# Two edits to a decoder-step kernel: query products of the even layer turned round, and expert panels parted by the contraction

## What is computed

```
q_in = qc * jnp.exp(b)
o_inter = jnp.einsum('bchk,bhkv->bchv', q_in, S)
att = jnp.einsum('bthk,bshk->bhts', q_in, k_in)
o_intra = jnp.einsum('bhts,bshv->bthv', att, vc)
return S_new, o_inter + o_intra
```

## Time and profile before

| | |
|---|---|
| median of 3 runs | 1671.39 us (1671.09 to 1671.58) |
| the profiled execution, own time | 1670.99 us |
| its span, first to last instruction | 1669.2 us |
| PE busy | 1587.6 us (95%) |
| DVE, ACT, POOL busy | 539.7, 341.4, 144.6 us |
| mean granted TensorE clock | 0.983 |
| mean DMA rate | 321 GB/s |

### The profile page before, as it was taken

The page is one execution under the profiler, slowest core; times in us unless marked ns, Lnnn a source line. Parts: engine busy times, 40 slices in busy tenths (PEclk is TensorE's granted clock), DMA queues, the critical chain, the costliest instruction groups (busy, mean ns, idle before and its releaser), DMA issues.

```text
span 1669.2 us, 21844 instructions
## 1 busy us (share of the span) xinstructions
PE 1587.6 (95%) x7954; PEld 799.2 (48%) x7954; DVE 539.7 (32%) x1322; ACT 341.4 (20%) x693; POOL 144.6 (9%) x221
## 2 busy tenths in 40 slices
PE   8999899999999999999999999989999999999998
PEld 5784544334344433446665755554443434443343
DVE  2145722222222222261434245372222222222225
ACT  2102122121122221231222222012212112221122
POOL 0330100000000000000011111010000000000000
PEclk9969999999999999999999999989999999999999
DMA  9623779999989999955385586577999998999970
GB/s 299 245 82 133 277 313 419 421 421 420 420 348 421 420 420 420 388 200 188 134 269 195 196 279 235 202 310 306 421 421 421 420 419 362 420 421 419 421 291 29
DMA packets 119271, 536.09 MB, mean 321 GB/s; under 512 B 17849, under 2 KB 29369, under 8 KB 69408
## 3 DMA queue, kind: packets, MB, share of 16 engines
q1 hardware_dynamic: 95975, 470.35, 70.5%
q0 software_dynamic: 21360, 61.64, 10.2%
q10 hardware_dynamic: 1872, 3.22, 0.6%
HBM read 526.15 MB, written 23.87 MB: 330 GB/s over the span
## 4 chain that ended last, share of the span: by engine, by line
PE 81%; DMA 11%; DVE 3%; issue 2%; ACT 1%; SPq 1%; POOL 0%; ACTq 0%; DVEq 0%
PE ps L1252 23%; PE ps L1116 12%; PE ps L1094 12%; DMA weights<-in_w_exp_up 11%; PE ps L1266 10%; PE ps L1228 5%; PE ps L1245 3%; PE ps L1224 2%; PE ps L1259 1%; PE ps L1010 1%; PE ps L1105 1%; PE ps L1286 1%; PE ps L988 1%; PE ps L901 1%; PE ps L1001 1%
## 5 line engine op out<-in xcount | busy, mean ns | idle before, releaser
L1252 PE MATMUL ps<-weights,x_feat 128*64 128x512 f32 x1984 | 437.8, 593 | 36.8 <-DMA weights<-in_w_exp_up 18.5
L1252 PEld LDWEIGHTS ps<-weights,x_feat 128*64 128x64 f32 x1984 | 147.1, 137 | 320.9 <-issue 318.2
L1266 PE MATMUL ps<-weights,arena 128*64 128x512 f32 x992 | 226.5, 598 | 0.9 <-ACT arena L1450 0.9
L1094 PE MATMUL ps<-x_feat,weights 128*128 128x288 f32 x832 | 210.2, 411 | 1.1 <-ACT x_feat L1450 1.1
L1094 PEld LDWEIGHTS ps<-x_feat,weights 128*128 128x128 f32 x832 | 159.9, 194 | 45.1 <-issue 3.8
L2104 DVE CAST split<-state 128x1024 fp32r<-128x1024 f32 (+1 forms) x66 | 44.7, 678 | 324.9 <-ACT state L1450 324.9
L2101 DVE SCALAR_TENSOR_TENSOR arena<-arena,ps 128x256 f32<-128x256 f32 x64 | 30.7, 480 | 365.3 <-ACT arena L1679 365.3
L2423 POOL DMA_INDIRECT arena<-x_rows,arena x64 | 63.6, 993 | 891.0 <-DVE arena L2094 845.9
L1450 ACT ACTIVATE state<-ps 128x512 f32<-128x512 f32 x132 | 78.8, 597 | 268.5 <-PE ps L1266 261.1
L1116 PE MATMUL ps<-weights,x_feat 128*128 128x512 f32 x288 | 126.7, 594 | 3.0 <-ACT x_feat L1476 3.0
L1266 PEld LDWEIGHTS ps<-weights,arena 128*64 128x64 f32 x992 | 65.7, 136 | 132.3 <-issue 130.9
(11 more groups left out here) (289 smaller groups left out, 1280.8 us busy)
## 6 DMA issues: line engine op xcount, KB each, us to landing
weights<-in_w_exp_gate SPq DMA_DIRECT2D x124, 1024.0 KB, 14.8
weights<-in_w_exp_up SPq DMA_DIRECT2D x124, 1024.0 KB, 18.8
weights<-in_w_exp_down SPq DMA_DIRECT2D x124, 1024.0 KB, 16.9
weights<-in_w_in_c SPq DMA_DIRECT2D x24, 1024.0 KB, 8.1
arena<-in_state_ret POOLq DMA_DIRECT2D x20, 512.0 KB, 5.5
out_ret_sample<-arena POOLq DMA_DIRECT2D x20, 512.0 KB, 6.5
weights<-in_w_in_a SPq DMA_DIRECT2D x8, 1024.0 KB, 10.9
weights<-in_w_ple_gate SPq DMA_DIRECT2D x8, 1024.0 KB, 17.8
```

The costliest lines, as they stand in the source:

```text
L1094: last = pe.matmul(ps[:, 0:T], lhs(c), XT[:, c, :], start=(c == 0), stop=(c == n - 1))
L1252: last = pe.matmul(ps[64 * s:64 * s + 64, :], XGT[u][:, c, 64 * s:64 * s + 64], rhs, start=(c == 0), stop=(c == KC - 1))
L1266: last = pe.matmul(ps[64 * s:64 * s + 64, :], HT[u][:, c, 64 * s:64 * s + 64], wd[s][:, c, 512 * n:512 * n + 512], start=(c == 0), stop=(c ...
```

## The change

Two parts.

**A, even layer.** The queries of a chunk become the stationary operand (QI is laid out chunk by chunk, so that the 32 columns lie together) and the state the moving one, 128 columns. Four chunks write four strips of 32 output partitions of one bank. There are 32 such products for the prompt (the first chunk's state is set to zero by a POOL memset and takes part) and 16 for the samples: groups ("qS", 0), ("qS", 1), ("qSs"). ACT copies each bank to SBUF (for the samples with a factor 0 or 1 for each row, from a new table column `own_strip`). The pooling products follow. Then ("oT", f) takes its four products of scores and values and four more of 128 x 128 by the identity, which turn the copied result and add it; ("oTs") takes its four and four more with a folding matrix.

**B, expert loop.** For the first and the last pair of each layer, panels 0 and 1 hold the first and the second half of the contraction of all four matrices, in runs of 4 KB where the other panels have 8 KB. `gate_up_halves` waits for one panel, does 8 products, waits for the next, does 8 more. At the first pair it signals after the first half, and SP refills that slot then. SP's first loop iteration is written out for this.

```diff
+            g.extend((("qS", 0), ("qS", 1), ("qSs",)))
+            g.extend(("pool", f) for f in range(4))
             g.extend((("oT", 0), ("oT", 1), ("oTs",)))
-            g.extend(("pool", f) for f in range(4))
...
+                def contraction_panel(num, e0, k):
+                    s = slot_full[num % SLOTS]
+                    dst = wp(num).rearrange("p (s m x) -> p s m x", s=2, m=2)
+                    for m, w in enumerate((A["w_exp_gate"], A["w_exp_up"])):
+                        src = w[l, e0:e0 + 2].rearrange("e (p c) n -> p e (c n)", c=KC)
+                        sp.dma_start(dst[:, :, m, :], src[:, :, 1024 * k:1024 * k + 1024]).then_inc(s, 16)
...
                             if k == 2:
                                 sp.wait_ge(bank_full[1], base[1] + 3 * (u - 1 + late) + 6 * it)
+                            elif isinstance(it, int) and it == 1 and u + k == 0:
+                                sp.wait_ge(sem("half_consumed"), l + 1)
                             else:
                                 sp.wait_ge(bank_full[0], base[0] + 2 * (u + late) - 3 + 4 * it)
-                            expert_panel(n0 + 3 * u + k, 4 * it + 2 * u, k)
+                            if isinstance(it, int) and it > 1 and k < 2:
+                                contraction_panel(n0 + 6 * it + k, 4 * it, k)
+                            else:
+                                expert_panel(n0 + 3 * u + k, 4 * it + 2 * u, k)
...
             for f in range(2):
-                for i in range(1, NCA):
-                    pe.matmul(out2[:, :, CA * i:CA * i + CA], SS[:, f, i, :], QI[:, f, :, CA * i:CA * i + CA],
-                              start=(i == 1), stop=False, skip_group_check=True)
+                ps = begin(("qS", f))
+                for i in range(NCA):
+                    q, g = i % 4, i // 4
+                    last = pe.matmul(ps[TS * q:TS * q + TS, P * g:P * g + P], QI[:, f, i].rearrange("p k c -> p (k c)"), SS[:, f, i, :],
+                                     start=(g == 0), stop=(g == 3), skip_group_check=True)
+                end(last, ("qS", f))
...
             for f in range(2):
+                out2 = begin(("oT", f)).rearrange("p (k t) -> p k t", k=2)
...
+                emptied(pe, ("qS", f))
+                for g in range(4):
+                    tokens_of = out2[:, :, 64 * g:64 * g + 64].rearrange("p k (i c) -> p i k c", c=CA)
+                    last = pe.matmul(tokens_of, QS[f][:, P * g:P * g + P], ident, start=False, stop=(g == 3),
+                                     skip_group_check=True)
                 end(last, ("oT", f))
...
+            emptied(pe, ("qSs",))
+            for f in range(2):
+                for g in range(2):
+                    last = pe.matmul(out4[:, 2 * f:2 * f + 2, CA * g:CA * g + CA], QSS[:, P * (2 * f + g):P * (2 * f + g) + P],
+                                     fold_all[:, 0:TS], start=False, stop=(f == 1 and g == 1), skip_group_check=True)
             end(last, ("oTs",))
...
+                def gate_up_halves(u, ring, it, ps):
+                    for k in range(2):
+                        n = ring + k
+                        pe.wait_ge(slot_full[n % SLOTS], 32 * (n // SLOTS + 1) + 32 * it)
+                        w = wp(n).rearrange("p (s m c n) -> p s m c n", s=2, m=2, c=4)
+                        for c in range(4):
+                            for s in range(2):
+                                last = pe.matmul(ps[64 * s:64 * s + 64, :], XGT[u][:, 4 * k + c, 64 * s:64 * s + 64],
+                                                 w[:, s, :, c, :], start=(k == 0 and c == 0), stop=(k == 1 and c == 3))
+                        if it == 0 and k == 0:
+                            last.then_inc(sem("half_consumed"), 1)
+                    return last
...
+                    for f in range(2):
+                        full(act, ("qS", f))
+                        st.free(copy(QS[f], bank(("qS", f))), ("qS", f))
+                    full(act, ("qSs",))
+                    st.free(copy(QSS, bank(("qSs",)), scale=own_strip), ("qSs",))
```

More of the change, by code:

```diff
@@ L430, in trunk @@
         AT = XTb[:, 4 * T:8 * T].rearrange("p (h t) -> p h t", h=4)
+        QS = [STATE[:, 512 * f:512 * f + 512] for f in range(2)]
+        QSS = keys[:, 0:512]
         a = Cut(AR[:, :], ASZ)
@@ L763, in _, with two_pairs @@
                         wait_slot(n0 + 3 * pr + k)
-                        expert_panel(n0 + 3 * pr + k, 2 * pr, k)
+                        if pr == 0 and k < 2:
+                            contraction_panel(k + n0, 0, k)
+                        else:
+                            expert_panel(n0 + 3 * pr + k, 2 * pr, k)
                 sp.wait_ge(sem("flag_ready"), l + 1)
                 go = sp.value_load(flagi[0:1, 0:1], min_val=0, max_val=1)
-                def two_pairs(it, late):
-                    for u in range(1 if isinstance(it, int) else 2):
+                def two_pairs(it, late, pairs=2):
+                    for u in range(pairs):
                         for k in range(3):
@@ L887, in even_pe @@
                 for j, (o, r) in enumerate(CH):
-                    last = pe.matmul(ps[0:r, o:o + r], KI[:, h // 2, o:o + r], QI[:, h // 2, h % 2, o:o + r],
-                                     start=True, stop=True)
+                    last = pe.matmul(ps[0:r, o:o + r], KI[:, h // 2, o:o + r],
+                                     QI[:, h // 2, o // CA:(o + r) // CA, h % 2, :], start=True, stop=True)
                 end(last, ("att", h))
@@ L1316, in two_pairs @@
                             pe.wait_ge(sem("home_in"), 96 * (l + 1))
-                        else:
+                        elif not (first or last):
                             for n in range(ring, ring + 2):
@@ L1320, in two_pairs @@
                         pe.wait_ge(bank_free[0], base[0] + uses(0, pr, 0))
-                        gate_up(u, HOME_UP if home else [wp(ring), wp(ring + 1)], PS[:, 0, :]).then_inc(bank_full[0], 1)
+                        if first or last:
+                            gate_up_halves(u, ring, it, PS[:, 0, :]).then_inc(bank_full[0], 1)
+                        else:
+                            gate_up(u, HOME_UP if home else [wp(ring), wp(ring + 1)], PS[:, 0, :]).then_inc(bank_full[0], 1)
                         pe.wait_ge(bank_free[1], base[1] + uses(1, pr, 0))
@@ L1792, in even_dve @@
                         dve.wait_ge(sem("queries_zeroed"), 1)
-                    st.run(STT(QI[0:64, f, 0, :], ps[0:64], DKA ** -0.5, EB[0:64, f, :], ALU.mult, ALU.mult))
-                    st.free(STT(QI[64:128, f, 1, :], ps[64:128], DKA ** -0.5, EB[64:128, f, :], ALU.mult, ALU.mult), ("qk", f))
+                    for k in range(2):
+                        rows = slice(64 * k, 64 * k + 64)
+                        ins = STT(QI[rows, f, :, k, :], ps[rows].rearrange("p (i c) -> p i c", c=CA), DKA ** -0.5,
+                                  EB[rows, f, :].rearrange("p (i c) -> p i c", c=CA), ALU.mult, ALU.mult)
+                        if k:
+                            st.free(ins, ("qk", f))
+                        else:
+                            st.run(ins)
                 else:
@@ L2328, in even_pool @@
             store(O["pool_sample"][0, :, 0:PBUF - DSEQ, :], A["state_pool"][0, :, DSEQ:PBUF, :], s)
+            st.run(pool.memset(SS[:, :, 0, :], 0.0))
+            st.after
             st.tell(pool.memset(QI, 0.0), sem("queries_zeroed"))
```

35 lines of the change are left out of this document (19 added, 16 removed).

## The result

The changed kernel takes 1656.95 us (median of 4 runs, 1655.94 to 1657.13), the kernel before 1671.24 beside it: a ratio of 0.991, interval 0.990 to 0.993. The forecast was 1649.0 with a range to 1655.5: the direction is right, but 8 us of the 22.4 are missing. The profiled execution took 1657.13 us, span 1655.2 (before 1669.2).

The account below looks back on a forecast made before the run. PE bounds nearly all; in the expert loop the weight stream's start does. 13.1 + 2 x 3.1 + 1.6 + 1.5 = 22.4 us off 1670.99 gives 1648.6, plus 0.4: 1649.0 us, range 1646.5 to 1655.5.

Parts of the forecast that it names:

- Part A: Even layer, query products to oTs: products turned round in strips, with pooling and folds, gain 13.1 us.
- Rival 2: Even layer: the clock returns early, around 107 us, 1.4 us better, 1647.6 us; chance 10%.
- The copies: Even layer: ACT's three copies of 0.60 us each, done at 110.3 before the first fold needs them, cost nothing.
- First pair: Expert loop's start: refill issued 3.5 us earlier, gain 3.1 us a layer, between 0 and 3.5.
- Rival 3: Expert loop: the stream runs dry at 230.7 us, losing the early refill's gain; 6.2 us worse, 1655.2 us; chance 13%.
- Last pair: Expert loop's end: gate_up starts without idle time before it, gain 1.6 us, and 1.5 in layer 1.
- the sum: Whole kernel: 13.1 + 2 x 3.1 + 1.6 + 1.5 = 22.4 us gained, all reaching the end.
- What was to show it wrong: Pooling starting after 112 us, clock 0.50 at the output projection, or home pair's gate_up less than 2 us earlier.
- rivals outside the range (4 and 5): Clock stays low after the even layer's products, 1687.7 us, 2%; strips don't overlap and extra folds cost, 1665 us, 5%.
- theory 1: Posed after the result: at layer 0's loop end PE waits for its own instructions at the overflow branch, about 7 us.
- theory 4: Posed after the result: three added groups shift later PSUM banks, costing time before layer 0's loop and at the odd layer.

Follow-up runs that it names:

- e11: Changed kernel with 48 instructions less in TensorE's never-entered overflow routine, so only the branch's target moves; 1650.50 us, ratio 0.988.
- e1: Changed kernel without TensorE's branch over the overflow routine and the routine's body; 1650.44 us, ratio 0.988 to the kernel before.
- e7: Kernel before with 56 instructions (112 waits on the second constant transfer) at the head of TensorE's program; 1696.31 us, ratio 1.016.
- e15: Changed kernel with PSUM banks turned back by five at layer 0's router and 32 instructions of waits in PE's idle time ahead of it; 1647.08 us, ratio 0.985.
- e8: Changed kernel with banks turned back at the output projection and 64 instructions (waits on the second constant transfer) at the program's head; 1667.22 us, ratio 0.998.
- e9: Changed kernel with banks turned back at layer 0's router and 64 instructions (waits on the identity's semaphore) at the program's head; 1651.90 us, ratio 0.989.
- e13: Changed kernel with PSUM banks turned back by five at layer 0's router, nothing else; 1653.63 us, ratio 0.989 to the kernel before.
- e5: Changed kernel with the PSUM bank rotation skipping five at the first group of the output projection; 1655.13 us, ratio 0.991 to the kernel before.
- e3: Kernel before with the even layer's part of the change alone; 1665.88 us, ratio 0.996.
- e12: Changed kernel with the prompt's query products ordered four behind each other in one strip instead of round the strips; 1659.19 us, ratio 0.993.
- e10: Changed kernel with 32 instructions (waits on the identity's semaphore) at the head of TensorE's program; 1651.05 us, ratio 0.989.
- e2: Kernel before with 256 no-ops at the head of TensorE's overflow routine, which the compiler dropped; 1671.31 us, ratio 1.000.

## Why the prediction was wrong

- **Part A.** Right in place and mechanism, low by 2.8 us. The products took 4.04 us, not 5.9: the 32 for the prompt took 3.17, where doubling L1111's time at the full clock gave 3.9, and the samples' sixteen ran at the risen clock, 0.87 for 2.0. Pooling 2.14 (2.0 forecast), oT 3.56 (4.3, since at the full clock a 128-column product behind others is 0.22 us, not 0.27), oTs 2.01 (2.1). Rival 2, the early clock with 1.4 us, is what happened in the profiled execution. That part is luck: in the thirteen traces with this even layer the clock came back 2.4 to 5.3 us after the first strip product (2.7 here, 5.0 in e11 at 109.4, nearly the 109.3 of the forecast), and in e11 the stretch from there to the output projection took 14.9 us against 13.8 here, 29.5 before and 16.4 forecast. PE was as busy in L901 as in L922, and only in the second did the clock come back. The Trainium skill's sentence that "activity releases the throttle" (TensorE: Matmul & The Clock Gate, Part 1) fits the one and not the other.
- **The copies.** ACT's three take 0.60 to 0.69 us and are done at 108.4; the folds start at 110.6. The warning of the Trainium skill that the prediction cites (TensorEngine Tiling (Array Packing), Performance Considerations), of a PSUM copy as the bottleneck, did not come true, as forecast.
- **First pair.** 3.15 and 2.55 us against 3.1 each. SP issues 3.7 us after the first gate_up starts, where it waited for its end in the earlier trace rows, and the stream is at 429 GB/s from 203.3 to 208 us; from 212 to 220 it dips to 355. Rival 3, the lost refill, is out. Timeline of SP in the changed kernel:

```profile
199.88 0.33 SPq L738 DMA_DIRECT2D weights<-in_w_exp_gate  x1
...
203.31 0.33 SPq L738 DMA_DIRECT2D weights<-in_w_exp_gate  x1
...
209.83 0.80 SPq L738 DMA_DIRECT2D weights<-in_w_exp_down  x2
```

- **Last pair.** 1.7 and 1.4 us against 1.6 and 1.5. The last gate_up has no idle time before it, unlike the earlier trace rows, and none at its middle (7.04 us for all 32). PE's timeline:

```profile
662.97 7.04 PE L1297 MATMUL ps<-weights,x_feat 128*64 128x512 f32 x32
```

- **The step that failed is the sum.** It adds what each stage gains and lets all of it reach the end: "All loads of the expert phase wait for oTs or for later ends, so they move along", and of the chain behind oTs "Both move with oTs, so the slack stays". I followed engines, queues and transfers, and put at nothing, without a reason, two things that the change moves without touching them: which bank a later group gets, and where PE's later code lies. The second is the larger: 4.85 us of idle and 2.4 by the clock (e1, e7, e11). The first came with 2.0 us before the loop in the profiled execution, by the low clock that followed the longer wait in four of seven traces, and perhaps 1 at the odd layer's start. 22.4 + 2.8 (even layer) - 0.5 (pairs) - 2.0 - 7.3 - 1.3 = 14.1, and 14.05 was measured. With both undone the kernel takes 1647 to 1648 us, 1 to 2 below the forecast.
- **What was to show it wrong** named only places of the change itself, and none of them did. Its list of chances puts 7% on the rivals outside the range (4 and 5), not the 13% that it states.

Of theory 1, what is shown: the gap comes and goes with the place of the branch and its target alone (e1, e7, e11, e15), and PE goes on 1.8 to 1.9 us after the page packet ends in all six kernels that have it. That the page behind the target is asked for only as the branch lands is a reading: it fits every place tried, but not the two products counted ahead of the page's end, and no run shows the request itself. The Trainium skill (Runtime: NRT & Kernel Launch, Instruction fetch mechanics) has pages of 16 KiB read in sequence, and a stall for a taken branch that leaves a window of two pages. The pages' size agrees with the packets. The stall here came with a target that is on the very next page by the compiled count (target 254 instructions behind the branch), so by that rule there should have been none; by the reading above the page after it was the late one. In layer 1 the target lies 134 instructions ahead of its page's end, and there is no gap. Of theory 4, the odd layer's share is less firm: its first block took 17.2 to 17.7 us with the banks turned back (e8, e9, e13 to e15) and 17.9 to 18.7 without (18.15 in the changed kernel). With the banks of the kernel before (and in e5, e13 and e15) PE's idle time before it comes in two pieces of 0.78 and 0.44 us, in the changed kernel in one of 1.35. But e5 has the same banks as e13 from the router on and took 15.77 us, since its clock did not fall there; so the size hangs on the clock.

## What to carry to other kernels

- When a change adds PSUM groups or instructions, look past its own stage: list which bank each later group gets before and after, and where each taken branch lands in its 16-KB page. Both can be read before a run, and here each was mended by a line or two.
- A branch over a long routine that is never entered isn't free. Its target wants to be well ahead of a page's end; the runs show this only where the DMA engines are full. Idle time of "issue" that no semaphore explains, with a packet of the instruction queue in it, is the sign.
- A wait that is moved or lengthened can cost nothing or several times itself, by whether the clock falls behind it. Read that off several traces before giving it a price.
- In a sum of gains, check at each later stage that the shift is still there; a table of shifts like the one above finds a loss in minutes.

## What the runs showed of the hardware

- The idle time at the branch was 4.6 to 5.5 us, with the DMA engines full (after, e3, e5, e7, e12, e13), and the projection behind it took 8.6 to 10.1 us at a clock of 0.50 for a part of it, against 6.87: 1.7 to 3.3 us more.
- PE's program is read ahead of what runs: in e10 the next page's packet starts 6.2 us ahead of the branch, though PE runs through the 22 instructions between its own page's start (by the count) and the branch in 1.2 us.
- 128 waits in 64 instructions at the head of PE's program put the first product at 9.78 us instead of 5.2 to 6.3 (e9); 64 waits in 32 instructions were hidden there (e10: 6.22) and in an idle time of 3.95 us (e15). No-ops take nothing, since they are not in the compiled program (e2).
- A product of 32 stationary and 128 moving columns costs 99 ns when neighbours go to different strips and some 200 ns when four stand one behind the other in a strip, mostly at half clock (L922 in the changed kernel and in e12).
- The same strip products had the clock back at 1.00 after 2.4 us in one trace and after 5.3 us in another (e1, e8).
